# A routed mixture-of-experts encoder block: routing per chunk, column compares for the index tables, and a third output copy for the last three items

## The reference, cut to what matters

```
xn  = rms_norm(x);  z = xn @ W_in                          # 1024 x 1536
A   = spatial gating of gelu(z[:, :1024]);  B = Re(2-D DFT of z[:, 1024:])
h   = x + concat(rms_norm(A), rms_norm(B)) @ W_out
hn  = rms_norm(h)
s   = sigmoid(hn @ w_router)                               # 64 experts in 8 groups of 8
pick: add the bias, keep the 4 groups with the largest sum of their two best, then the top 8
gate = 2.5 * s / sum of the picked s
out = h + sum over the picked experts e of gate_e * (silu(hn Wg_e) * (hn Wu_e)) Wd_e
        + (silu(hn Sg) * (hn Su)) Sd                       # the shared expert
y   = rms_norm(out)
```

## Time and profile before

| | |
|---|---|
| median of three runs | 1428.37 us |
| the profiled execution | 1429.72 us, of it 1428.0 us between its first and last instruction |
| granted TensorE clock, mean | 0.963 of full speed |
| TensorE busy / VectorE / ScalarE / GpSimd | 1315.2 / 851.2 / 738.2 / 452.0 us |
| DMA | 339.54 MB, 238 GB/s over the span |

### The profile page before, as it was taken

One profiled execution on the slowest core, in us unless ns is written; L12 is line 12 of the kernel. 1 busy time (PEld: TensorE's weight loads), 2 busy tenths in 40 slices (PEclk: granted clock), 3 DMA queues, 4 the chain that ended last, 5 costly groups with the idle time before them and its releaser, 6 DMA issues.

```text
span 1428.0 us, 25654 instructions
## 1 busy us (share of the span) xinstructions
PE 1315.2 (92%) x5961; PEld 1027.9 (72%) x5962; DVE 851.2 (60%) x1144; ACT 738.2 (52%) x1044; POOL 452.0 (32%) x608
## 2 busy tenths in 40 slices
PE   6999988999969899999999999899999999999970
PEld 4885466887434688888878888787877788888860
DVE  4530543333555567767786667775587756676835
ACT  4321244221010467767775656675677766676742
POOL 1431201000001244444433434344343434343434
PEclk9999999998978999999999999999999999999995
DMA  9504022113104789999999999999899998999949
GB/s 332 169 9 158 15 104 89 45 45 157 57 0 148 254 255 367 325 292 317 337 368 293 267 273 272 372 323 295 270 338 365 359 268 268 336 328 277 304 94 367
DMA packets 88269, 339.54 MB, mean 238 GB/s; under 512 B 12976, under 2 KB 23216, under 8 KB 71472
## 3 DMA queue, kind: packets, MB, share of 16 engines
q1 hardware_dynamic: 60880, 254.73, 46.0%
q0 software_dynamic: 27360, 84.44, 26.4%
HBM read 290.66 MB, written 66.85 MB: 250 GB/s over the span
## 4 chain that ended last, share of the span: by engine, by line
PE 70%; DMA 13%; DVE 4%; issue 4%; ACT 3%; DVEq 2%; SPq 1%; ACTq 1%; POOL 1%; POOLq 0%
PE ps L683 26%; PE ps_out L697 13%; DMA raw_gu<-in_w_up 7%; PE ps L583 6%; PE ps L451 5%; PE ps L434 5%; PE ps L618 4%; PE ps L485 4%; DMA raw_dn<-in_w_down 3%; PE ps L534 2%; ACT w_gu L882 2%; PE ps L628 1%; PE ps_out L600 1%; DVE w_gu L1135 1%; PE ps L705 1%
## 5 line engine op out<-in xcount | busy, mean ns | idle before, releaser
L683 PE MATMUL ps<-w_gu,xTh 128*128 x1504 | 479.6, 400 | 12.5 <-DVE xTl L1252 10.6
L1135 DVE TENSOR_TENSOR w_gu<-raw_gu,w_gu (+1 forms) x256 | 302.5, 1222 | 68.2 <-ACT w_gu L882 65.4
L683 PEld LDWEIGHTS ps<-w_gu,xTh 128*128 128x128 f32 x1504 | 280.2, 191 | 72.5 <-issue 17.8
L683 PE MATMUL ps<-w_gu,xTl 128*128 x752 | 297.2, 395 | 0.0
L882 ACT ACTIVATE w_gu<-raw_gu (+1 forms) x256 | 256.8, 1059 | 25.9 <-SPq L380 25.8
L697 PE MATMUL ps_out<-w_dn,hTh 128*128 x744 | 242.0, 406 | 0.8 <-DVE hTl L1257 0.8
L1435 POOL DMA_INDIRECT y_rows_dram<-ob,idxs x93 | 151.4, 1628 | 195.6 <-ACT ob L903 185.7
L1142 DVE TENSOR_TENSOR w_dn<-raw_dn,w_dn (+1 forms) x128 | 151.0, 1220 | 77.3 <-ACT w_dn L886 77.0
L683 PEld LDWEIGHTS ps<-w_gu,xTl 128*128 128x128 f32 x752 | 143.1, 190 | 30.1
L697 PEld LDWEIGHTS ps_out<-w_dn,hTh 128*128 128x128 f32 x744 | 133.2, 189 | 26.0 <-issue 0.9
L697 PE MATMUL ps_out<-w_dn,hTl 128*128 x372 | 146.1, 393 | 0.0
(11 more groups left out here) (199 smaller groups left out, 1536.0 us busy)
## 6 DMA issues: line engine op xcount, KB each, us to landing
raw_gu<-in_w_gate SPq DMA_DIRECT2D x64, 1024.0 KB
raw_gu<-in_w_up SPq DMA_DIRECT2D x64, 1024.0 KB
raw_dn<-in_w_down SPq DMA_DIRECT2D x64, 1024.0 KB
y_rows_dram<-zero SPq DMA_DIRECT2D x1, 4608.0 KB, 18.8
y_rows_dram<-xh SPq DMA_DIRECT2D x9, 512.0 KB, 11.4
x_ring<-in_x SPq DMA_DIRECT2D x8, 512.0 KB, 4.8
w_in_sb<-in_w_in SPq DMA_DIRECT2D x8, 512.0 KB, 10.1
xh<-in_x SPq DMA_DIRECT2D x8, 512.0 KB, 7.3
```

The lines of the kernel that those rows point to most:

```text
L683: mm = pe.matmul(ps[3][:, :], x_[:, k, :], w_gu[:, bass.ds(at, 1), part, :, k, :], start=(k == 0 and part == 0 and x_ is xTh), stop=(k == ...
L1135: dv.tensor_tensor(gu_part(w_gu[:, :, 1, :, :, :], at, m), gu_part(raw_gu, at, m), gu_part(w_gu[:, :, 0, :, :, :], at, m).bitcast(F32), AL ...
```

## The change

1. **Input**: POOL's wait for the small loads moves behind `rstd` of chunk 2. The zeroed region in DRAM grows from one copy to two, with the dump block zeroed by a small DMA.
2. **Routing** runs per chunk, in VectorE's output-stage loop: `route(c - 2)` after the scaled rows of chunk c, the last two behind it.
3. **Tables**: `hit`, `mark` and `pick` become 8 + 8 tensor_scalar instructions on one [128, 136] or [128, 128] row each, all in 16-bit floats, with one wait for the sixteen.
4. **TensorE's order** in the shared expert: each small routing matmul has one more gate-up product ahead of it or behind it, and the eight table groups stand in pairs between the last gate-up products; `s_down` waits for the last shared product in place of the tables, and uses other banks. VectorE's last shared product comes behind the tables.
5. **Handover to the items**: the two first stores stand ahead of the third expert's load, the ninth store is gone, ScalarE waits only for the first four stores and VectorE for all eight.
6. **End**: the last three items add to a third copy, one after another. Copies 1 and 2 are loaded once every earlier add has landed and the weight slots are free; after the last add only copy 3 is loaded, and a second sum (`last_copy`) adds it. The final norm's weights are loaded at the handover.

```diff
@@ SyncE
-            load_next_gu(2, 1)
             gu_landed(0, 1)
             dn_landed(1, 1)
-            for c in range(NC):
+            def store_y0(c):
                 sp.wait_ge(s_y0, c + 1)
-                sp.dma_start(yv[c], xh[:, c, :]).then_inc(s_yst, 16)
-            sp.dma_start(yv[NC], xh[:, 0, :]).then_inc(s_yst, 16)
+                sp.dma_start(yv[c], xh[:, c, :]).then_inc(s_yst[c // 4], 16)
+            store_y0(0)
+            store_y0(1)
+            load_next_gu(2, 1)
+            for c in range(2, NC):
+                store_y0(c)
+            sp.wait_ge(s_idx, 2)
+            sp.dma_start(gf_row[:, :], spread(gf, D)).then_inc(s_gf, 16)
...
+            sp.wait_ge(s_hg, NE * GU_PARTS)
+            sp.wait_ge(s_lg, NE * GU_PARTS)
+            sp.wait_ge(s_hd, NE * KF)
+            sp.wait_ge(s_ld, NE * KF)
...
+            for u in range(TURN):
+                sp.wait_ge(s_add[u], before_last * 16)
+            for c in range(NC):
+                sp.dma_start(ya_in[:, c, :], yv[c]).then_inc(s_x[c], 16)
+                if c < NC // 2:
+                    sp.dma_start(yb_in[0][:, c, :], yv2[c]).then_inc(s_x[c], 16)
+            sp.wait_ge(s_gu, last + 1)
+            for c in range(NC // 2, NC):
+                sp.dma_start(yb_in[1][:, c - NC // 2, :], yv2[c]).then_inc(s_x[c], 16)
             n = turns(sp)
             for u in range(TURN):
                 sp.wait_ge(s_add[u], n * 16)
             for c in range(NC):
-                sp.dma_start(xh[:, c, :], yv[c]).then_inc(s_yl[c], 16)
-                sp.dma_start(yb_in[:, c, :], yv2[c]).then_inc(s_yl[c], 16)
-                if c == 0:
-                    sp.dma_start(gf_row[:, :], spread(gf, D)).then_inc(s_gf, 16)
+                sp.dma_start(yc_in[:, c, :], yv3[c]).then_inc(s_yl[c], 16)
@@ TensorE
             s_gate_up(0, 0)
-            s_gate_up(0, 1)
...
-            s_gate_up(1, 0)
+            s_gate_up(0, 1)
             pe.wait_ge(s_chunks, 1)
...
             s_gate_up(1, 1)
             s_gate_up(2, 0)
+            table(0)
+            table(1)
             s_gate_up(2, 1)
+            table(2)
+            table(3)
             s_gate_up(3, 0)
+            table(4)
+            table(5)
             s_gate_up(3, 1)
+            table(6)
+            table(7)
...
-            pe.wait_ge(s_idx, 2)
@@ ScalarE
             split_gu(1, range(GU_PARTS))
+            act.wait_ge(s_rd, 1)
+            split_dn(1)
             act.wait_ge(s_tab, 1)
             second = expert(1)
             evac_xT(0)
-            act.wait_ge(s_hm, 4)
-            act.wait_ge(s_gst, 16)
-            act.wait_ge(s_rd, 1)
-            split_dn(1)
-            act.wait_ge(s_yst, 16 * (NC + 1))
+            act.wait_ge(s_yst[0], 16 * 4)
@@ VectorE
+            def route(c):
+                dv.wait_ge(s_sc, c + 1)
+                r = c % 2
+                step(dv.tensor_tensor(rt_a[:, c, :], scores[:, c, :], rb_row[:, :], ALU.add))
+                many(dv.max(m8[:, r, g, :], rt_a[:, c, g * GE:(g + 1) * GE]) for g in range(NG))
...
+                step(dv.tensor_tensor(mask[:, c, :], rt_a[:, c, :], rt_b[:, c, :], ALU.not_equal))
...
+                if 2 <= c:
+                    route(c - 2)
+            route(NC - 1)
             dv.sem_inc(s_mask, 1)
...
-                step(dv.tensor_tensor(hit[:, :, :], count_row[:, None, :].to_broadcast([P, TOPK, TAB]),
-                                      item8[:, c, :, None].to_broadcast([P, TOPK, TAB]), ALU.is_equal))
-                dv.tensor_scalar(mark[:, c % 2, :, :], hit[:, :, :], token[:, c:c + 1], None, ALU.mult).then_inc(s_rv, 1)
-                step(dv.tensor_tensor(pick[:, c % 2, :, :], count_row[:, None, 1:P + 1].to_broadcast([P, TOPK, P]),
-                                      place8[:, c, :, None].to_broadcast([P, TOPK, P]), ALU.is_equal))
+                marks = [dv.tensor_scalar(mark[:, c % 2, k, :], count_row[:, :], item8[:, c, k:k + 1], token[:, c:c + 1],
+                                          ALU.is_equal, ALU.mult) for k in range(TOPK)]
+                picks = [dv.tensor_scalar(pick[:, c % 2, k, :], count_row[:, 1:P + 1], place8[:, c, k:k + 1], None,
+                                          ALU.is_equal) for k in range(TOPK)]
+                many(marks + picks)
...
             rest_dn(1, 0)
+            dv.wait_ge(s_yst[0], 16 * 4)
+            dv.wait_ge(s_yst[1], 16 * 4)
...
+            def last_copy(c):
+                dv.wait_ge(s_both, c + 1)
+                dv.wait_ge(s_yl[c], 16)
+                dv.tensor_tensor(ya_in[:, c, :], ya_in[:, c, :], yc_in[:, c, :], ALU.add).then_inc(s_sum, 1)
+            for c in range(NC):
+                both_copies(c)
+            last_copy(0)
+            last_copy(1)
@@ GpSimd
-            gp.wait_ge(s_small, 16 * 9)
             for step_ in range(NC + 1):
...
+                if step_ == 1:
+                    gp.wait_ge(s_small, 16 * 9)
...
-                if u < 2:
+                if same_copy and u > 0:
+                    gp.wait_ge(s_add[u - 1], 16 * turn + 16)
+                elif u < 2:
                     after(gp, s_add[u + 1], 16 * turn)
...
-            with gp.Fori(1, turns(gp)) as t:
+            with gp.Fori(1, turn) as t:
                 turn_of_items(t)
-            add_rows(last, TURN - 1, turn)
+            turn_of_items(two_less + 1, same_copy=True)
+            add_rows(last, TURN - 1, turn, same_copy=True)
```

More of the change, by code:

```diff
@@ L195, in build @@
         tab = place("tab", [2, TAB], I32)
-        ends = place("ends", [1, 4], I32)
+        ends = place("ends", [P, 8], I32)
+        late = place("late", [P, 1], F32)
         mhalf = place("mhalf", [P, 1], F32)
@@ L212, in sem @@
             return ctx.enter_context(nc.semaphore(name))
-        s_x = [sem(f"x_in{c}") for c in range(NC)]
+        s_x = [sem(f"rows_in{c}") for c in range(NC)]
         s_wi = [sem(f"w_in_uv_in{k}") for k in range(KD)]
@@ L1286, in y0 @@
                 dv.wait_ge(s_sdn, c + 1)
-                for half in range(2):
+                for half, bank in enumerate(((0, 4), (6, 7))[c % 2]):
                     piece = xh[:, c, half * 512:(half + 1) * 512]
-                    ins = dv.tensor_tensor(piece, ps[4 + 2 * (c % 2) + half][:, :], piece, ALU.add)
+                    ins = dv.tensor_tensor(piece, ps[bank][:, :], piece, ALU.add)
                 ins.then_inc(s_y0, 1)
```

207 lines of the change are left out of this document (113 added, 94 removed).

## The result

The changed kernel took **1412.57 us** (median of 4 runs, 1406.10 to 1413.97) where the kernel before, run beside it, took 1428.88 (1427.68 to 1432.48): ratio 0.9864, 95% interval 0.9842 to 0.9887. It is faster, by 16 us and not by the 31 forecast, and 3.6 us above the upper end of the range. The profiled execution took 1411.65 us (span 1410.0), 18.07 less than that of before (1429.72). So 12.6 us of the forecast 30.65 are to be found. Two more profiles of the same kernel stand beside it; the columns show what varies from one execution to the next.

What follows compares the result with a forecast made beforehand. TensorE was taken to bound most of the span, so work went to four places where it idles. Gains 2.4 + 16.1 + 2.8 + 4.65 + 2.5 + 2.2 = 30.65 us take 1428.37 to 1397.7 us; range 1391 to 1409.

Steps and rivals of the forecast that it cites:

- the gain of the start: Input: chunk 2's `rstd` no longer waits for small loads, so chunk 1's products start at 30.2 us; gain 2.4 us.
- the gain of the end: After the last down product: last add lands 3 us later, first scale comes 5.1 us sooner; gain 2.2, bounds 5 and -3.
- routing and tables: Shared expert: early mask and tables hidden beside gate-up products, so `s_down` starts at 416.0 in place of 432.10; gain 16.1 us.
- clock of `s_down`, handover: `s_down` keeps full clock, gain 2.8 us; at the handover to the items TensorE waits less for stores, gain 4.65 us.
- clock of item 1's product: Its 24 matmuls run at full clock, 5.46 us as in later items in place of 7.96; gain 2.5, bound 0.
- item stretch: The items, left alone by the change: everything through the last down product moves with them, no gain of their own.
- a rival's case: Short gaps at `s_down` and item 1: the clock falls, losing one or both of 2.8 and 2.5 us; chance 0.22.
- The rival that had loads holding up two chained adds: End: 8.4 MB of loads delay two chained adds by 5 us each or more; 1401 to 1407 us, chance 0.10.
- The rivals' other conditions: Items slowed by the weight stream, say 10 us (chance 0.07); compares not hidden, from 0.25 us each (chance 0.07).
- both clock losses: The 2.8 us at `s_down` and 2.5 us at item 1's product both lost; the rival's 1400 to 1403 us, chance 0.22.
- the slow compares: Tables: compares at 0.36 us each make the three pairs late, 11 us; rival's range 1398 to 1409 us, chance 0.07.

Runs made afterwards that it cites:

- e9: The changed kernel run again with no edit: median 1409.32 us, ratio 0.9871 to the kernel before.
- e2: The changed kernel with the load of x's chunk 3 issued after five of the nine small loads: median 1408.00 us, ratio 0.9851 to the kernel before.
- e16: The changed kernel a third time, with no edit: one execution, 1412.36 us.
- e6: The changed kernel with routing over all eight chunks at once behind the output stage, as before: median 1418.97 us, ratio 0.9917 to the kernel before.
- e4: The changed kernel with the early loads of copies 1 and 2 held until all adds but the last have landed: median 1420.31 us, ratio 0.9941 to the kernel before.
- e8: The changed kernel with all eight last sums ahead of the scales and GpSimd's roots in two groups of four: median 1405.70 us, ratio 0.9827.
- e3: The changed kernel with the old end, two output copies loaded behind the last add: median 1406.90 us, ratio 0.9838 to the kernel before.
- e11: The changed kernel with the edits of e2 and e7 and the old end of e3: median 1400.56 us, ratio 0.9796 to the kernel before.
- e12: The changed kernel with four unread products on TensorE in the pauses around the first item's turn: median 1405.45 us, ratio 0.9829 to the kernel before.
- e7: The changed kernel with VectorE's wait for the stores moved behind the first gated product: median 1408.33 us, ratio 0.9839 to the kernel before.
- e10: The changed kernel with the edits of e2, e7 and e8 together: median 1399.12 us, ratio 0.9787 to the kernel before.

## Why the prediction was right and wrong

The sign and the main term were right, the time was not: the steps that failed are the gain of the start and the gain of the end, forecast at 2.4 and 2.2 us and measured as losses of 3.3 and 3.6. Point by point, in the profile, forecast and measured gain:

| term | forecast | measured | short |
|---|---|---|---|
| start (to the end of the output stage) | 2.4 | -3.3 | 5.7 |
| routing and tables | 16.1 | 16.1 | 0 |
| clock of `s_down`, handover | 2.8 + 4.65 | 6.3 | 1.1 |
| clock of item 1's product | 2.5 | 0.8 | 1.7 |
| item stretch | 0 | 1.7 | -1.7 |
| end | 2.2 | -3.6 | 5.8 |
| sum | 30.65 | 18.0 | 12.6 |

**Start, wrong.** Chunk 1's products came at 29.82 (forecast 30.2). The step that failed is "Gain 2.4 us": it was read off chunk 1 and carried to the end without asking what the next chunk needs. ScalarE's chain to it, a square that waits for a load, the table load, the copy and the rounding, had 0.7 us of slack in the kernel before, less than the 2.4 that were to be gained. Even with the load at its early time (e9) z_a gains only 1.2 us; in ten profiles of twelve the load was also late, and TensorE's clock fell in the pause. e2 shows both gone. The term also had no lower bound, so a loss here was nowhere in the range.

**Routing and tables, right.** A route took 3.54 us (346.53 to 350.07, forecast 3.5), and `s_down` starts 16.1 us earlier once the 3.3 us by which the last sum of the output stage begins late (341.87 against 338.58) are taken off (15.8 in e9, 16.0 in e16). That the forecast's 16.1 is met to the tenth is partly luck: `route(5)`, which stands ahead of the last copy to T, delays the first gate-up product by some 0.6 us (354.34 against 350.47, less the 3.3), not by 0.1. The compares follow each other after 0.20 us, above the 0.14 taken, below the 0.25 from which they would count. The rule of the Trainium skill's "VectorE: DVE Perf Modes", "The TRN2 errata", would have had 0.30 and 9.5 us a pair; the trace has 6.55. A single `mark` does last 0.30 to 0.32 us from start to end, as in that estimate, but the next one starts after 0.23 us (`pick`: 0.25 and 0.16), so what adds up in an unbroken run is the spacing and not the duration. e6 bears out that without the early mask TensorE waits and `s_down` starts 5.8 us later.

**Handover and clock, half right.** The last store landed at 453.94, 0.2 us ahead of the turn's end where 0.7 was reckoned, so "the wait ends about when it is needed" held. But behind that wait stood 1.8 us up to the gated product, most of it register reads, that the sum did not have. The clock stayed up over 1.56 us of idle ahead of `s_down` (right, the 2.8), and fell in the pauses of 1.97 and 1.01 us ahead of item 1's product, a rival's case (chance 0.22, priced at 2.5; it cost 1.7). The 7.96 us of the kernel before were not matmuls at a falling clock, as the forecast says, but at one that had fallen and came back: they start at half pace (1.22 us for two) and end at full.

**End, wrong.** Two sizes (and a slip: 5.1 less 3 is 2.1, not 2.2). The adds: the last was put at 8.5 to 9 us and its predecessor left out of account; they took 9.08 and 10.44, so that the last is issued 3.2 us after it could have been and lands 14.3 us after the last down product instead of 8.4: 5.9 us, 3 forecast. The rival that had loads holding up two chained adds by 5 us each (chance 0.10) names the mechanism; they lost 4.1 and 2.7. e4 shows that the loads do it. And the scales: "the other seven at today's pace, 16.5 us for seven", took 18.5, for the forecast counted one of GpSimd's two steps. In the kernel before they took 0.94 and 1.45 us, and VectorE ran beside them all but without a pause, a chunk in 2.56 us; now they take 1.31 and 1.40, VectorE idles 0.46 us ahead of each scale, and a chunk takes 2.88. The first scale came 8.8 us after the landing (forecast 8.0).

The 1.7 us gained in the items were not forecast and lie within that stretch's spread over the profiles (895.7 to 900.6); no run gives them a cause. The rivals' other conditions did not come about: the items' stretch did not get longer, and no compare was late.

The range, 1391 to 1409, let the losses come one at a time: both clock losses end at 1403, the slow compares at 1409. What came were four at once, the start, the end, one clock and the handover, and of the 12.6 us 11.5 are the start and the end.

## What to carry to other kernels

When a wait is taken away at the start of a pipeline, the gain is worth only the slack of the next engine's chain to the next chunk: read that slack off the old trace, its loads included, before carrying the gain to the end. Loads moved ahead to "lie beside" small chained DMAs stretched each of these by 40 to 80% here, so read off what else of the path is in the queues then before an early load is counted as a gain. And a small step on GpSimd between two VectorE instructions can take as long as the instruction it runs beside (0.22 us alone, up to 1.3 here); count every such step on the path, and try them gathered in one group, as e8 did.

## What the runs showed of the hardware

- **An accumulating add beside loads**: 9.0 to 11.5 us in all profiles with the third copy, but for the one that e4 kept free of loads (6.4 at most); 6.25 to 6.46 alone in the kernels with two copies (before, e3, e11). The "twice its transfer time" that the prediction drew from the Trainium skill's "DMA: Bandwidth & Descriptors" can't be split off from these; 1.4 to 1.8 times in all does not speak against it.
- **GpSimd beside VectorE**: a [128, 1] step takes 0.22 us alone (0.57 with `pow`) and up to 1.3 (1.4) us beside VectorE's instructions of 1.22 and 1.28 us on [128, 1024] tiles in SBUF. The Trainium skill's "GPSIMD Engine Reference", "Specifications", says that GpSimd's way to SBUF is shared with VectorE where its instruction has two SBUF inputs, which is the case for both; the trace agrees. The pace of the scales varies with how the two fall together: 2.88 us a chunk in the changed kernel, 2.33 in e12 (first steps of 0.71 us in place of 1.31), with the same instructions.
- **TensorE's clock**: it stayed at 2.4 GHz over the 1.5 to 1.6 us of idle ahead of `s_down` in all seventeen profiles with the new order. At item 1 it fell to 1.2 GHz in the profiles with two pauses (1.7 to 2.4 and 0.8 to 1.0 us) and in two of three with one (7.36 us for the product behind a pause of 1.72 in e7, 7.34 behind 1.72 in e10, but 5.73 behind 1.75 in e11), and stayed with the pauses filled (e12). The same pause was followed by either level.
- **The same kernel's start** has two forms: the square behind chunk 3's load starts at 33.2 or at 35.5 to 35.6 us, and `s_down` at 415.6 or at 419.3 to 419.6.
